# Gate and up products of a SwiGLU by feature instead of by token: activations stream past stationary weights

## The chip, the cores and the metric

The kernel runs on one core of one Trainium2 chip. The metric is the time on the device in microseconds of one execution. Three runs of the kernel before took 2477.77, 2479.46 and 2479.61 us, so the median is 2479.46 us.

## What is computed

A decoder trunk of two layers on 256 tokens of width 2048, all in float32: an RWKV-7 time mixing layer, then an attention layer (here one block of 256 keys), and after each of them a SwiGLU feed-forward part of width 5632 between two layer norms. The change is in the feed-forward part, which runs twice:

```python
def _swiglu(x, w_gate, w_up, w_down):
    return (jax.nn.silu(x @ w_gate) * (x @ w_up)) @ w_down

for layer in range(DEPTH):                      # DEPTH = 2
    mixed = time_mix(h, ...) if layer < 1 else attention(h, ...)
    h = _layernorm(ALPHA * h + mixed, ln1_w[layer], ln1_b[layer])
    h = _layernorm(ALPHA * h + _swiglu(h, ffn_w_gate[layer], ffn_w_up[layer], ffn_w_down[layer]), ln2_w[layer], ln2_b[layer])
```

## The kernel before

**Products in three parts.** The type float32r lets TensorE take a float32 product in one pass, at less than float32's precision. Each operand is therefore split in a high part (a cast to float32r) and a low part (the rest), and a product is three matmuls: high activations by high weights, high by low, low by high. Activations lie in `ahi` and `alo` ([128, 16 k tiles, 256 tokens]), weights come through a ring of four slots, `raw` (from memory), `whi` and `wlo`.

**Jobs and chunks.** A job makes 512 output columns for both tiles of 128 tokens from all k tiles. A chunk is two k tiles of it (256 x 512 weights, 512 KB), so a gate or up job has 8 chunks. For every chunk, SP issues the DMA into `raw` (L343, L344), ACT casts it to `whi` (`split_hi`, L1270), DVE makes `wlo` (`split_lo`, L1713), and TensorE runs `chunk` (L593 to L604): per k tile and token tile three matmuls of 512 columns, L601 to L603, 12 in a chunk and 96 in a job. The stationary operand, which is loaded again for every matmul, is a 128 x 128 tile of activations, and the weights stream past it. ACT may cast chunk c+4 once TensorE is through with chunk c (`chunk_used`); TensorE waits for `split_done`; SP refills a slot of `raw` once its `wlo` is made. Jobs alternate between two sets of accumulators in PSUM (parity 0: banks 0 and 1, parity 1: banks 2 and 3); `bank_free[parity]` hands a set back.

**The feed-forward part** (`ffn`, on TensorE L1118 to L1146, on ACT L1567, on DVE L2135). The width of 5632 is cut in 11 blocks of 512. Each block is a gate job (parity 0), then an up job (parity 1). ACT takes Silu of the gate sums into `gtmp` (L1577, L1588), DVE multiplies it by the up sums in PSUM (`multiply`, L2143). The result has tokens on the partitions, but the product with `w_down` wants features there: `h_transposes` (L1122 to L1128) turns it with 8 transposes of 128 x 128 (L1127) into banks 4 and 5, after the next block's gate job. ACT casts it into `hThi` (`hidden_hi`, L1573) and DVE subtracts for `hTlo` (`hidden_lo`, L2147). The last block's transposes stand inside the first down job. The order on each engine is the order in the code, and blocks 1 to 10 are a hardware loop of 10 rounds.

**The first gate job** (`normed_job`, L1078) starts while the layer norm is still being finished. Its first three chunks (`plain`, L1092 to L1101) are true float32 matmuls from `raw` and `hF`, the normed activations; each shows as two records of TensorE in the trace. `hF` is what ACT writes (L1544) from transposes (L1089), and DVE splits it into `ahi` and `alo` (`split_act`, L2099, L2100). The other five are ordinary chunks. `normed_job` also opens the products for the keys.

Of the kernel before, what the change touches and what calls it, by code (L numbers as in the profile page):

```python
# [23 lines left out]
F32 = mybir.dt.float32  # L24
# [5 lines left out]
P = 128  # L30
# [126 lines left out]
def trunk(nc, x, rows, rwkv_rows, lora, w, consts, ln_rows, y):  # L157
    with ExitStack() as ctx:
# [25 lines left out]
        ahi = sb("ahi", [P, KT, T], F32R)  # L184
        alo = sb("alo", [P, KT, T], F32R)
# [87 lines left out]
        hF = carve(a2t, KT * T, KT, T)  # L273
        gtmp = carve(common, 32 * KB, TT, NB)
# [3 lines left out]
        spare = alo.rearrange("p (s k m) t -> p s k (m t)", s=RING, k=KC)  # L278
# [51 lines left out]
        h_tr, hhi_done, hlo_done = (sem(n) for n in ("h_tr", "hhi_done", "hlo_done"))  # L330
# [259 lines left out]
        def _(pe):  # L590
# [15 lines left out]
            def job(c, u, parity, kt, hi, lo):  # L606

                pe.wait_ge(bank_free[parity], u + 1)
                for ch in range(kt // KC):
                    chunk(c, ch, parity, kt, hi, lo)  # L610

# [466 lines left out]
            def normed_job(n, name):  # L1078
# [13 lines left out]
                def plain(t, ch):  # L1092
# [19 lines left out]
                for ch in range(PLAIN, CJ):  # L1112
                    pe.wait_ge(ln_hi, n * CJ + ch - PLAIN + 1)
                    chunk(c, ch, 0, KT, ahi, alo)
                pe.wait_ge(ln_hi, (n + 1) * CJ)
                job(c + CJ, j // 2, 1, KT, ahi, alo)

            def ffn(layer):  # L1118
# [3 lines left out]
                def h_transposes(i):  # L1122

                    pe.wait_ge(bank_free[1], i + (j0 // 2 + 2 - u0))
                    for f in range(4):
                        for t in range(TT):
                            last = tr(ps[:, 4 + f // 2, (f % 2) * T + t * P:(f % 2) * T + (t + 1) * P], gtmp[:, t, f * P:(f + 1) * P], ident[:])  # L1127
                    last.then_inc(h_tr, 1)  # L1128

                normed_job(2 * layer, f"up{layer}")  # L1130
# [8 lines left out]
                for ch in range(CF):  # L1139
# [3 lines left out]
                    if ch == 1:  # L1143
                        h_transposes(u0 + FB - 1)
# [4 lines left out]
            normed_job(1, "kvq")  # L1149
# [106 lines left out]
        def _(act):  # L1256
            A = nc.scalar.activation

            def split_hi(c, u, n):

                for ch in range(n):
# [305 lines left out]
            def ffn(layer):  # L1567
                c0, _ = PH[f"up{layer}"]
                u0 = layer * FB

                def hidden_hi(i, f0):
                    act.wait_ge(h_tr, i + 1)
                    A(hThi[:, f0, :], ps[:, 4:6, :].rearrange("p a (k t) -> p (a k) t", k=2), ACT.Copy).then_inc(hhi_done, 1)  # L1573
# [3 lines left out]
                A(gtmp, ps[:, 0:2, :], ACT.Silu).then_inc(bank_free[0], 1)  # L1577
# [3 lines left out]
                with act.Fori(0, FB - 1) as i:  # L1581
                    c = i * (2 * CJ) + (c0 + 2 * CJ)
                    u = i * (2 * CJ // RING) + (c0 + 2 * CJ) // RING
                    split_hi(c + RING, u + 1, CJ)

                    act.wait_ge(h_tr, i + (u0 + 1))
                    act.wait_ge(chunk_used, c + CJ)
                    A(gtmp, ps[:, 0:2, :], ACT.Silu).then_inc(bank_free[0], 1)  # L1588
                    hidden_hi(i + u0, bass.ds(i * 4, 4))
                    split_hi(c + (RING + CJ), u + (1 + CJ // RING), CJ)  # L1590
                c = PH[f"down{layer}"][0] + RING
                split_hi(c, c // RING, 1)
                hidden_hi(u0 + FB - 1, slice((FB - 1) * 4, FB * 4))
# [86 lines left out]
        def _(dve):  # L1680
# [26 lines left out]
            def split_lo(c, n, s0=0):  # L1707

                for ch in range(n):
# [425 lines left out]
            def ffn(layer):  # L2135
# [3 lines left out]
                def multiply(c_end, up_seen):  # L2139
# [140 lines left out]
```

## Time and profile before

| | |
|---|---|
| median of three runs | 2479.46 us |
| the profiled execution | 2478.32 us |
| its span, first to last instruction | 2476.4 us |
| TensorE matmul busy | 2444.3 us, 99% of the span, 15550 records |
| TensorE weight load busy | 2002.6 us, 81%, 15550 records |
| VectorE (DVE) busy | 1410.4 us, 57% |
| ScalarE (ACT) busy | 1074.2 us, 43% |
| GpSimd (POOL) busy | 129.9 us, 5% |
| HBM traffic | 440.88 MB, mean 178 GB/s |
| granted TensorE clock | 0.998 of full speed |

The profiled execution took 1.9 us more than its span and 1.1 us less than the median. The recorded duration of a matmul holds its way through the array, and matmuls overlap, so a matmul of 512 columns that is recorded with 389 ns does not cost 389 ns. What it costs is the pitch, the distance from one start to the next. Where a row of the timeline holds several instructions of one line (xN), its length is N-1 pitches and one duration.

### The profile page before, as it was taken

What the parts mean: (1) busy time and instruction counts of PE and PEld (TensorE: products, weight loads), DVE (VectorE), ACT (ScalarE), POOL (GpSimd) and SP (SyncE); (2) the same over time, 40 slices, a digit from 0 to 9 for tenths busy, and PEclk for the clock granted to TensorE, in tenths of its full rate; (3) what the DMA queues carried; (4) which work ended last, traced back from release to release, by engine and by line L of the source; (5) the groups of instructions that cost most, each with busy time, mean ns of one, the idle gap of its engine ahead of it and who ended that gap; (6) DMA issues with size and microseconds to landing.
All of it is one profiled execution on the core that took longest, in us unless ns stands there. A gap on an engine that the chain in (4) does not pass through costs nothing.

```text
span 2476.4 us, 39453 instructions
## 1 busy us (share of the span) xinstructions
PE 2444.3 (99%) x15550; PEld 2002.6 (81%) x15550; DVE 1410.4 (57%) x1743; ACT 1074.2 (43%) x1348; POOL 129.9 (5%) x172
## 2 busy tenths in 40 slices
PE   8999999999999999999999999999999999999997
PEld 6888787877888888888887888888788888888886
DVE  7788566676744444454446644566744444454445
ACT  4454355444444444443334444453544444444332
POOL 2000235420000000000000000000000000000000
PEclk9999999999999999999999999999999999999999
DMA  7556411265666666666665665445566666666654
GB/s 235 188 193 207 126 42 39 70 209 190 192 190 189 188 191 186 189 188 193 194 195 199 204 193 189 140 169 184 178 187 188 193 187 188 186 199 216 192 194 141
DMA packets 225884, 440.88 MB, mean 178 GB/s; under 512 B 13616, under 2 KB 24240, under 8 KB 224672
## 3 DMA queue, kind: packets, MB, share of 16 engines
q1 hardware_dynamic: 221760, 417.38, 54.3%
q0 software_dynamic: 3600, 21.55, 2.6%
q8 instruction: 92, 1.51, 0.3%
q10 hardware_dynamic: 400, 0.18, 0.0%
q14 instruction: 32, 0.26, 0.0%
HBM read 436.96 MB, written 2.10 MB: 177 GB/s over the span
## 4 chain that ended last, share of the span: by engine, by line
PE 95%; DMA 2%; DVE 1%; ACT 1%; issue 1%; POOL 0%; SPq 0%; DVEq 0%; ACTq 0%
PE ps L601 26%; PE ps L603 26%; PE ps L602 26%; PE ps L914 3%; PE ps L1099 1%; PE ps L797 1%; PE ps L807 1%; PE ps L1127 1%; PE ps L629 1%; PE ps L628 1%; PE ps L630 1%; PE ps L904 1%; PE ps L858 1%; PE ps L762 1%; PE ps L941 1%
## 5 line engine op out<-in xcount | busy, mean ns | idle before, releaser
L1270 ACT CAST whi<-raw 128x1024 fp32r<-128x1024 f32 x735 | 772.8, 1052 | 1146.8 <-PE ps L603 1087.9
L1713 DVE TENSOR_TENSOR wlo<-raw,whi 128x1024 fp32r<-128x1024 f32 x549 | 670.3, 1225 | 615.8 <-ACT whi L1270 613.7
L601 PE MATMUL ps<-whi,ahi 128*128 128x512 f32 x2172 | 851.3, 392 | 0.0
L603 PE MATMUL ps<-whi,alo 128*128 128x512 f32 x2172 | 845.6, 389 | 0.0
L602 PE MATMUL ps<-wlo,ahi 128*128 128x512 f32 x2172 | 845.1, 389 | 0.0
L603 PEld LDWEIGHTS ps<-whi,alo 128*128 128x128 f32 x2172 | 407.6, 188 | 85.7
L602 PEld LDWEIGHTS ps<-wlo,ahi 128*128 128x128 f32 x2172 | 407.9, 188 | 84.3 <-issue 1.0
L601 PEld LDWEIGHTS ps<-whi,ahi 128*128 128x128 f32 x2172 | 407.8, 188 | 84.1 <-DVE alo L2100 0.7
L2045 DVE TENSOR_TENSOR wlo<-raw,whi 128x1024 fp32r<-128x1024 f32 x193 | 236.2, 1225 | 249.6 <-ACT whi L1270 247.5
L601 PE MATMUL ps<-whi,hThi 128*128 128x512 f32 x656 | 255.4, 389 | 0.0
L603 PE MATMUL ps<-whi,hTlo 128*128 128x512 f32 x656 | 255.2, 389 | 0.0
L602 PE MATMUL ps<-wlo,hThi 128*128 128x512 f32 x656 | 255.2, 389 | 0.0
L601 PEld LDWEIGHTS ps<-whi,hThi 128*128 128x128 f32 x656 | 123.1, 188 | 25.7
L602 PEld LDWEIGHTS ps<-wlo,hThi 128*128 128x128 f32 x656 | 123.1, 188 | 25.5
L603 PEld LDWEIGHTS ps<-whi,hTlo 128*128 128x128 f32 x656 | 123.1, 188 | 25.4
L914 PE MATMUL ps<-raw,big 128*128 128x256 f32 x256 | 68.0, 398 | 0.6 <-issue 0.5
L577 POOL DMA_DIRECT2D big<-ln_rows x3 | 1.6, 537 | 1113.1 <-PE ps L630 786.9
L914 PEld LDWEIGHTS ps<-raw,big 128*128 128x128 f32 x256 | 44.7, 189 | 8.5 <-issue 1.3
L1544 ACT ACTIVATE a2t<-ps,lnT 128x128 f32<-128x128 f32 x96 | 34.2, 497 | 33.2 <-PE ps L1089 33.2
L1876 DVE TENSOR_TENSOR rec<-ps,big 128x512 f32<-128x512 f32 x40 | 27.6, 689 | 36.4 <-PE ps L797 36.4
L1721 DVE SCALAR_TENSOR_TENSOR big<-big,mixT 128x256 f32<-128x256 f32 x96 | 40.7, 480 | 0.5
L2147 DVE TENSOR_TENSOR hTlo<-ps,hThi 128x1024 f32 (+1 forms) x22 | 26.9, 1225 | 19.5 <-ACT hThi L1573 19.5
(317 smaller groups left out, 1942.3 us busy)
## 6 DMA issues: line engine op xcount, KB each, us to landing
raw<-w_up SPq DMA_DIRECT2D x176, 512.0 KB, 3.6
raw<-w_down SPq DMA_DIRECT2D x176, 512.0 KB, 3.9
raw<-w_gate SPq DMA_DIRECT2D x170, 512.0 KB, 3.6
raw<-w_k SPq DMA_DIRECT2D x32, 512.0 KB, 3.9
raw<-w_r SPq DMA_DIRECT2D x32, 512.0 KB, 4.4
raw<-w_v SPq DMA_DIRECT2D x32, 512.0 KB, 4.1
raw<-w_o SPq DMA_DIRECT2D x32, 512.0 KB, 4.9
raw<-kv_v SPq DMA_DIRECT2D x32, 512.0 KB, 3.7
```

Source lines behind the costliest of these rows:

```text
L601: mm(o, hi[:, k, tok], whi[:, s, k2, :], start=(k == 0), stop=False)
L602: mm(o, hi[:, k, tok], wlo[:, s, k2, :], start=False, stop=False)
L603: last = mm(o, lo[:, k, tok], whi[:, s, k2, :], start=False, stop=(k == kt - 1))
L628: mm(ps[:, 2 + t, :], hi[:, k, tok], wh[:, k2, :], start=False, stop=False)
L914: last = mm(ps[:, 3, t * T:(t + 1) * T], xxT[:, k, t * P:(t + 1) * P], rawf[:, s, k % FK], start=(i == 0), stop=(k == KT - 1), skip_group_ ...
L1270: nc.scalar.copy(whi[:, s], src).then_inc(hi_done, 1)
L1544: ins = A(hF[:, k, t * P:(t + 1) * P], ps[:, 4 + b, k2 * P:(k2 + 1) * P], ACT.Identity, scale=lnT[:, (n * 2) * KT + k:(n * 2) * KT + k + 1 ...
L1713: V.tensor_tensor(wlo[:, s], src, whi[:, s].bitcast(F32), ALU.subtract).then_inc(split_done, 1)
L1721: return V.scalar_tensor_tensor(out=out, in0=xxT[:, k], scalar=mixT[:, m * KT + k:m * KT + k + 1], in1=xT[:, k, 1:T + 1], op0=ALU.mult, op ...
L1876: V.tensor_tensor(Z.rearrange("p l (j c) -> p l j c", c=CHUNK), ps[:, 0:2, 0:4 * CHUNK].rearrange("p l (j c) -> p l j c", c=CHUNK), mask_l ...
L2045: V.tensor_tensor(wl, raw[:, s], wh.bitcast(F32), ALU.subtract).then_inc(split_done, 1)
L2147: V.tensor_tensor(hTlo[:, f0, :], ps[:, 4:6, :].rearrange("p a (k t) -> p (a k) t", k=2), hThi[:, f0, :].bitcast(F32), ALU.subtract).then_ ...
```

## The change

In the gate and up jobs the roles are swapped. The stationary operand becomes a tile of 128 features of the weights, and the activations of all 256 tokens stream past it, so that features come out on the partitions and the transposes go. For this `ahi` and `alo` become two halves of one tensor `ahl` ([128, 16, 2, 256]): for each k tile the high and the low activations lie side by side. Per k tile and each of 4 feature tiles there are two matmuls (`turned_chunk`): `whi` by the run of 512 columns (high and low), and `wlo` by the 256 high columns, added onto the first half of the same bank. High and low sums stand in the two halves of a bank and are added later, so a job now fills four banks (parity 0: 0 to 3, parity 1: 4 to 7). ACT copies the low halves out (`keep_lo`), DVE adds the high halves (`gate_sum`, and the first line of `multiply`), ACT takes Silu in place, DVE multiplies. In the first gate job of each layer four banks are not free yet, so it works with 128 or 256 columns: `narrow_chunk` has three matmuls of 256 columns per feature tile, and `plain` has a float32 matmul of 128 columns per feature tile and token tile. The down, key, value, query, output and RWKV products keep the old form; only their activations lie in `ahl` now.

```diff
-        ahi = sb("ahi", [P, KT, T], F32R)
-        alo = sb("alo", [P, KT, T], F32R)
+        ahl = sb("ahl", [P, KT, 2, T], F32R)
+        ahi, alo = ahl[:, :, 0], ahl[:, :, 1]
...
-        hF = carve(a2t, KT * T, KT, T)
-        gtmp = carve(common, 32 * KB, TT, NB)
+        hF = carve(a2t, 0, KT, 2, T)[:, :, 1]
+        gtmp = carve(common, 32 * KB, FK, T)
+        low_half = carve(big, 80 * KB, FT, T)
...
+            def turned_chunk(c, ch, parity):
+                s = ch % RING
+                pe.wait_ge(split_done, c + (ch + 1))
+                for k2 in range(KC):
+                    k = ch * KC + k2
+                    for f in range(FK):
+                        o, cols = ps[:, 4 * parity + f, :], slice(f * P, (f + 1) * P)
+                        mm(o, whi[:, s, k2, cols], ahl[:, k].rearrange("p n t -> p (n t)"), start=(k == 0), stop=False, skip_group_check=True)
+                        last = mm(o[:, 0:T], wlo[:, s, k2, cols], ahi[:, k, :], start=False, stop=(k == KT - 1), skip_group_check=True)
+                last.then_inc(chunk_used, 1)
...
+            def narrow_chunk(c, ch):
...
+                    for f in range(FK):
+                        o, cols = ps[:, f // 2, (f % 2) * T:(f % 2 + 1) * T], slice(f * P, (f + 1) * P)
+                        mm(o, whi[:, s, k2, cols], ahi[:, k, :], start=False, stop=False, skip_group_check=True)
+                        mm(o, wlo[:, s, k2, cols], ahi[:, k, :], start=False, stop=False, skip_group_check=True)
+                        last = mm(o, whi[:, s, k2, cols], alo[:, k, :], start=False, stop=(k == KT - 1), skip_group_check=True)
...
-                        last = mm(ps[:, t, :], hF[:, k, tok], raw[:, ch, k2, :], start=(k == 0), stop=False)
+                        if by_feature:
+                            for f in range(FK):
+                                last = mm(ps[:, f // 2, (f % 2) * T + t * P:(f % 2) * T + (t + 1) * P], raw[:, ch, k2, f * P:(f + 1) * P], hF[:, k, tok],
+                                          start=(k == 0 and t == 0 and f % 2 == 0), stop=False, skip_group_check=True)
...
                 with pe.Fori(0, FB - 1) as i:
-                    job(i * (2 * CJ) + (c0 + 2 * CJ), i + (j0 // 2 + 1), 0, KT, ahi, alo)
-                    h_transposes(i + u0)
-                    job(i * (2 * CJ) + (c0 + 3 * CJ), i + (j0 // 2 + 1), 1, KT, ahi, alo)
-                    pe.wait_ge(hlo_done, i + (u0 + 1))
+                    turned_job(i * (2 * CJ) + (c0 + 2 * CJ), i + (j0 // 2 + 1), 0)
+                    turned_job(i * (2 * CJ) + (c0 + 3 * CJ), i + (j0 // 2 + 1), 1)
...
-                    if ch == 1:
-                        h_transposes(u0 + FB - 1)
...
+                def keep_lo(c_end, parity, f0, kept):
+                    act.wait_ge(chunk_used, c_end)
+                    nc.scalar.copy(low_half[:, f0, :], ps[:, 4 * parity:4 * parity + FK, T:2 * T]).then_inc(kept, 1)
...
                 with act.Fori(0, FB - 1) as i:
...
-                    split_hi(c + RING, u + 1, CJ)
-                    act.wait_ge(h_tr, i + (u0 + 1))
-                    act.wait_ge(chunk_used, c + CJ)
-                    A(gtmp, ps[:, 0:2, :], ACT.Silu).then_inc(bank_free[0], 1)
-                    hidden_hi(i + u0, bass.ds(i * 4, 4))
-                    split_hi(c + (RING + CJ), u + (1 + CJ // RING), CJ)
+                    keep_lo(c, 1, bass.ds(i * FK, FK), up_lo_kept)
+                    split_hi(c + RING, u + 1, 2)
+                    hidden_hi(i + u0, bass.ds(i * FK, FK))
+                    split_hi(c + RING, u + 1, CJ - 2, 2)
+                    keep_lo(c + CJ, 0, bass.ds(i * FK + FK, FK), gate_lo_kept)
+                    split_hi(c + (RING + CJ), u + (1 + CJ // RING), 2)
+                    act.wait_ge(bank_free[0], i + (j0 // 2 + 3))
+                    A(gtmp, gtmp, ACT.Silu).then_inc(silu_done, 1)
+                    split_hi(c + (RING + CJ), u + (1 + CJ // RING), CJ - 2, 2)
...
-                def multiply(c_end, up_seen):
-                    dve.wait_ge(bank_free[0], up_seen)
-                    dve.wait_ge(chunk_used, c_end)
-                    V.tensor_tensor(gtmp, gtmp, ps[:, 2:4, :], ALU.mult).then_inc(bank_free[1], 1)
+                def multiply(i, f0, ups):
+                    low = low_half[:, f0, :]
+                    dve.wait_ge(up_lo_kept, i + 1)
+                    V.tensor_tensor(low, ps[:, 4:4 + FK, 0:T], low, ALU.add).then_inc(bank_free[1], 1)
+                    dve.wait_ge(bank_free[1], ups)
+                    dve.wait_ge(silu_done, i + 1)
+                    V.tensor_tensor(gtmp, gtmp, low, ALU.mult).then_inc(h_made, 1)
+                def gate_sum(i, f0):
+                    dve.wait_ge(gate_lo_kept, i + (layer * (FB - 1) + 1))
+                    dve.wait_ge(hlo_done, i + (u0 + 1))
+                    V.tensor_tensor(gtmp, ps[:, 0:FK, 0:T], low_half[:, f0, :], ALU.add).then_inc(bank_free[0], 1)
...
                 with dve.Fori(0, FB - 1) as i:
                     c = i * (2 * CJ) + (c0 + 2 * CJ)
-                    multiply(c, i + (j0 // 2 + 2))
-                    split_lo(c + RING, CJ)
-                    hidden_lo(i + u0, bass.ds(i * 4, 4))
+                    multiply(i + u0, bass.ds(i * FK, FK), i + (j0 // 2 + 2))
+                    split_lo(c + RING, 2)
+                    hidden_lo(i + u0, bass.ds(i * FK, FK))
+                    split_lo(c + RING, CJ - 2, 0, 2)
+                    gate_sum(i, bass.ds(i * FK + FK, FK))
                     split_lo(c + (RING + CJ), CJ)
```

`turned_job` waits for `bank_free[parity]` and runs the 8 chunks of a job with `turned_chunk`.

## Rows read from the trace of the kernel before

**Rows 1.** The page, its head and first part: busy time by engine.
```profile
span 2476.4 us, 39453 instructions
PE 2444.3 (99%) x15550; PEld 2002.6 (81%) x15550; DVE 1410.4 (57%) x1743; ACT 1074.2 (43%) x1348; POOL 129.9 (5%) x172
```

**Rows 2.** The page, fourth part: the chain that ended last, by engine.
```profile
PE 95%; DMA 2%; DVE 1%; ACT 1%; issue 1%; POOL 0%; SPq 0%; DVEq 0%; ACTq 0%
```

**Rows 3.** The waits, longest first: engine, line, whom it waited for, us, times, longest.
```profile
ACT whi L1270 <- PE ps L603: 1087.9, 679, 3.1
DVE wlo L1713 <- ACT whi L1270: 614.8, 447, 4.7
```

**Rows 4.** Timeline, TensorE in a steady stretch: start us, length us, engine, line, instruction.
```profile
1000.01 0.39 PE L602 MATMUL ps<-wlo,ahi 128*128 128x512 f32 x1
1000.01 0.19 PEld L603 LDWEIGHTS ps<-whi,alo 128*128 128x128 f32 x1
1000.24 0.39 PE L603 MATMUL ps<-whi,alo 128*128 128x512 f32 x1
...
1007.94 0.39 PE L601 MATMUL ps<-whi,ahi 128*128 128x512 f32 x1
```

**Rows 5.** Timeline, TensorE around the transposes of two blocks that follow each other.
```profile
716.67 1.03 PE L1127 MATMUL ps<-ident,common 128*128 128x128 f32 x8
...
761.09 1.04 PE L1127 MATMUL ps<-ident,common 128*128 128x128 f32 x8
761.88 0.47 PE L601 MATMUL ps<-whi,ahi 128*128 128x512 f32 x1
762.20 0.39 PE L602 MATMUL ps<-wlo,ahi 128*128 128x512 f32 x1
...
764.28 0.39 PE L602 MATMUL ps<-wlo,ahi 128*128 128x512 f32 x1
```

**Rows 6.** One line's instructions, the transposes: count, durations in ns, first and last start.
```profile
L1127 PE MATMUL ps<-ident,common x176: 270/272/275, 672.3 to 2229.4; 128*128 128x128 f32 x176
```

**Rows 7.** Timeline, TensorE, float32 matmuls of 512, 256 and 128 columns.
```profile
251.01 1.02 PE L729 MATMUL ps<-big 128*128 128x512 f32 x2
...
277.63 2.76 PE L914 MATMUL ps<-raw,big 128*128 128x256 f32 x12
...
1546.72 0.38 PE L1172 MATMUL ps<-big 128*128 128x128 f32 x2
1546.94 0.60 PE L1173 MATMUL ps<-big 128*128 128x256 f32 x2
```

**Rows 8.** Groups by line and shape, weight loads: count, busy us, mean ns, idle before.
```profile
L601 PEld LDWEIGHTS ps<-whi,ahi 128*128 128x128 f32 x2172 | 407.8, 188 | 84.1 <-DVE alo L2100 0.7 <-issue 0.2
L1172 PEld LDWEIGHTS ps<-big 128*128 128x128 f32 x32 | 6.0, 189 | 1.0
```

**Rows 9.** Timeline, weight loads ahead of float32 matmuls of 2 columns (L732).
```profile
251.87 0.86 PEld L732 LDWEIGHTS ps<-big 128*128 128x128 f32 x7 [0.24 <-issue]
```

**Rows 10.** Timeline, ACT and DVE at the end of an up job.
```profile
741.75 1.21 DVE L2143 TENSOR_TENSOR common<-common,ps 128x1024 f32<-128x1024 f32 x1
742.24 1.06 ACT L1270 CAST whi<-raw 128x1024 fp32r<-128x1024 f32 x1 [1.67 <-PE ps L603]
743.33 1.23 DVE L1713 TENSOR_TENSOR wlo<-raw,whi 128x1024 fp32r<-128x1024 f32 x1 [0.37 <-ACT whi L1270]
...
744.96 1.05 ACT L1270 CAST whi<-raw 128x1024 fp32r<-128x1024 f32 x1 [1.66 <-PE ps L603]
```

**Rows 11.** The page, sixth part, one row: KB of a DMA and us from issue to landing.
```profile
raw<-w_up SPq DMA_DIRECT2D x176, 512.0 KB, 3.6
```

**Rows 12.** Timeline in the norm before the first gate job: float32 products, first split.
```profile
609.83 5.42 PE L1099 MATMUL ps<-raw,a2t 128*128 128x512 f32 x12 [0.29 <-ACT a2t L1544]
611.21 0.43 DVE L2099 CAST ahi<-a2t 128x512 fp32r<-128x512 f32 x1 [4.78 <-ACT a2t L1544]
611.67 0.69 DVE L2100 TENSOR_TENSOR alo<-a2t,ahi 128x512 fp32r<-128x512 f32 x1
```

More of the change, by code:

```diff
@@ L329, in trunk @@
         xhat_done, ln_tr, ln_aff, ln_hi, h_done = (sem(n) for n in ("xhat_done", "ln_tr", "ln_aff", "ln_hi", "h_done"))
-        h_tr, hhi_done, hlo_done = (sem(n) for n in ("h_tr", "hhi_done", "hlo_done"))
+        gate_lo_kept, up_lo_kept, silu_done, h_made, hhi_done, hlo_done = (
+            sem(n) for n in ("gate_lo_kept", "up_lo_kept", "silu_done", "h_made", "hhi_done", "hlo_done"))
         qk_tr, qkt_set, s_made, nm_set, p_set, p_normed, pt_made, pt_set, o_made, o_kept, ohi_set, olo_set, s_read = (
@@ L610, in job, with turned_job @@
                     chunk(c, ch, parity, kt, hi, lo)
+            def turned_chunk(c, ch, parity):
[8 more added lines that the diff above has]
+                last.then_inc(chunk_used, 1)
+            def turned_job(c, u, parity):
+                pe.wait_ge(bank_free[parity], u + 1)
+                for ch in range(CJ):
+                    turned_chunk(c, ch, parity)
+            def narrow_chunk(c, ch):
+                s = ch % RING
+                pe.wait_ge(split_done, c + (ch + 1))
+                for k2 in range(KC):
+                    k = ch * KC + k2
+                    for f in range(FK):
[3 more added lines that the diff above has]
+                        last = mm(o, whi[:, s, k2, cols], alo[:, k, :], start=False, stop=(k == KT - 1), skip_group_check=True)
+                last.then_inc(chunk_used, 1)
             def last_job(c, u, kt, hi, lo):
@@ L1113, in normed_job @@
                     pe.wait_ge(ln_hi, n * CJ + ch - PLAIN + 1)
-                    chunk(c, ch, 0, KT, ahi, alo)
+                    if by_feature:
+                        narrow_chunk(c, ch)
+                    else:
+                        chunk(c, ch, 0, KT, ahi, alo)
                 pe.wait_ge(ln_hi, (n + 1) * CJ)
-                job(c + CJ, j // 2, 1, KT, ahi, alo)
+                if by_feature:
+                    turned_job(c + CJ, j // 2, 1)
+                else:
+                    job(c + CJ, j // 2, 1, KT, ahi, alo)
             def ffn(layer):
@@ L1120, in ffn @@
                 u0 = layer * FB
[L1122 to L1130, printed above, removed]
+                normed_job(2 * layer, f"up{layer}", True)
                 with pe.Fori(0, FB - 1) as i:
-                    job(i * (2 * CJ) + (c0 + 2 * CJ), i + (j0 // 2 + 1), 0, KT, ahi, alo)
-                    h_transposes(i + u0)
-                    job(i * (2 * CJ) + (c0 + 3 * CJ), i + (j0 // 2 + 1), 1, KT, ahi, alo)
-                    pe.wait_ge(hlo_done, i + (u0 + 1))
+                    turned_job(i * (2 * CJ) + (c0 + 2 * CJ), i + (j0 // 2 + 1), 0)
+                    turned_job(i * (2 * CJ) + (c0 + 3 * CJ), i + (j0 // 2 + 1), 1)
                 c, j = PH[f"down{layer}"]
@@ L1257, in _, with split_hi @@
             A = nc.scalar.activation
-            def split_hi(c, u, n):
-                for ch in range(n):
+            def split_hi(c, u, n, at=0):
+                for ch in range(at, at + n):
                     s = (c + ch if isinstance(c, int) else ch) % RING
@@ L1705, in rsqrt, with split_lo @@
                     newton(dst, src, t)
-            def split_lo(c, n, s0=0):
-                for ch in range(n):
+            def split_lo(c, n, s0=0, at=0):
+                for ch in range(at, at + n):
                     s = (s0 + ch) % RING
```

28 lines of the change are left out of this document (16 added, 12 removed).

## The prediction

> **What bounds the kernel now.** I read the page from its head: TensorE is busy for 99% of the span, DVE for 57%, ACT for 43% [rows 1]. The chain that ended last lies on TensorE for 95% of the span [rows 2], and the longest waits are those of ACT for TensorE to be done with a slot, and of DVE for ACT [rows 3]: the two that prepare the weights are ahead. So the time is a count of TensorE's instructions times their pitch, and the pitch has to be read from starts, since recorded durations overlap.
>
> In a steady stretch 35 pitches lie between the first and the last start of [rows 4]: 7.93 / 35 = 0.2266 us for a float32r matmul of 512 columns. At the granted 2.4 GHz its 512 columns alone are 0.2133 us, so there are **13.3 ns on top**, which I call the overhead. Each such matmul has its own weight load, recorded with 0.19 us, which starts with the matmul before it [rows 4, 8]: the load lies fully beside a stream of 0.213 us. The block period, from one group of transposes to the next, is 761.09 - 716.67 = 44.42 us [rows 5]. Two jobs of 96 matmuls are 192 x 0.22667 = 43.52 us. What is left is 0.90 us; 8 transposes at (1.04 - 0.27) / 7 = 0.110 us are 0.88 of it [rows 5, 6]. Job ends and loop rounds cost TensorE nothing now.
>
> **What goes: the transposes.** All 176 [rows 6], in 22 groups, on the path: 22 x 0.90 = **19.8 us less**. They can't leave a hole that something else fills: what follows each is a matmul whose operands were ready (no idle stands in [rows 5]).
>
> **What is added: more, smaller matmuls.** The columns stay the same. A job before: 96 matmuls of 512, 49152 columns. After: 64 of 512 and 64 of 256, again 49152. But there are 128 matmuls and weight loads for 96, and half of the loads must hide behind a stream of 256 columns, 0.1067 us. 42 of the 44 gate and up jobs change so (all but the first gate job of each layer). No row has a float32r matmul of 256 columns, so its pitch is the unknown of this case, and nearly the whole answer.
>
> *Bounds.* From below: columns at the rate of the 512s, 0.2267 / 2 = 0.1133 us, that is all overhead going with columns. That is also about what a load needs: where matmuls of 2 columns follow each other, 7 loads take 0.86 us, (0.86 - 0.19) / 6 = 0.112 us each [rows 9]. The nearest rows for a load behind a stream of 0.107 us are the float32 matmuls of 128 columns, which stream each column in two cycles: two of them take 1546.94 - 1546.72 = 0.22 us, 0.110 each, with loads recorded as long as those of the float32r ones, 189 against 188 ns [rows 7, 8]. So load and stream still overlap when they are equally long. From above: the overhead is not always 13.3 ns. Behind the transposes, from 762.20 to 764.28, 9 pitches take 2.08 us, 0.2311 each, before they settle at 0.2267 [rows 5]: an overhead of 17.8 ns. If that stayed for every matmul, a 512 would cost 0.2311 and a 256 0.1245 us.
>
> *The value I take.* Float32 matmuls of 256 columns have a pitch of (2.76 - 0.38) / 11 = 0.2164 us for 0.2133 us of stream [rows 7], some 3 ns of overhead, with the same load beside them. So the rest of the 13.3 ns belongs to float32r, which reads a column of four bytes every cycle where float32 has two cycles for it. I read it as a price of each load that runs beside such a stream, since it moves after a change of what is loaded; a price of the load is the same for 256 columns as for 512. Then a 256 costs 0.1067 + 0.0133 = **0.1200 us**. I take the settled 0.2267 for the 512s, because steady stretches hold it over any change of slot and k tile.
>
> A turned job: 64 x (0.2267 + 0.1200) = 22.19 us for 96 x 0.2267 = 21.76, +0.43; 42 x 0.43 = **18.0 us more**. `narrow_chunk`: 24 x 0.1200 = 2.88 us for 12 x 0.2267 = 2.72, and there are 5 in each layer: 10 x 0.16 = **1.6 us more**. `plain`: now each of the two token tiles has 12 records of 512 columns [rows 12], with a pitch of 1.02 - 0.59 = 0.43 us as the two of L729 have it [rows 7] (0.59 is one record's duration), 5.16 us; after, 48 records of 128 columns at 0.110, 5.28. Two token tiles in two layers: **0.5 us more**.
>
> A rule of the Trainium skill (TensorE: Matmul & The Clock Gate, sections "Back-to-back issue gap" and "LDWEIGHTS (loading the stationary operand)") puts a warm matmul at N/2.4 + 2.5 ns and a load of 128 columns at 128/1.2 = 106.7 ns. It speaks softly against the change, as the load becomes as long as the stream of 256. For 512 columns the rule gives 215.8 ns and this trace shows 226.6 [rows 4], so for float32r the row decides. By the rule alone, for old and new matmuls alike, a pair would cost 1.3 ns more than its share of columns does now, 3.4 us in all, and the change would come out about where rival A has it.
>
> **What moves off TensorE.** On ACT a block gets two copies of 1024 elements out of PSUM beside Silu and cast, on DVE two additions. At 1.05 us for each on ACT and 1.23 on DVE, what 1024 elements cost there now, ACT has 20 x 1.05 = 21.0 us and DVE 20 x 1.23 = 24.6 us of work in a block of 44 [rows 10]. The tightest place is the end of an up job, t = 0. ACT casts chunk c+3 (to 1.05), copies the low half (2.1); DVE does `wlo` of c+3 (2.3), then adds (3.5) and, behind its wait for the sum and for Silu, multiplies (4.8). Queued behind these on DVE is `wlo` of chunk c+4, whose cast is ready at 2.72 + 1.05 = 3.8: done at 6.1, and TensorE wants it at 4 x 2.72 = 10.9. SP refills that slot 2.3 us later than now; the DMA lands in 3.6 us [rows 11], at 9.7, and ACT wants it at 13.6. The gate job's end is easier (one copy, one addition). The four new banks of a job are freed by that same addition, a whole job before they are wanted. So I cost all of it at nothing; if the cover were gone, each microsecond late would count at 42 job ends, 42 us. In the norm, `split_act` now writes two runs of 256 in place of one of 512. Its cast has 0.43 us for 512 elements [rows 12], less than the 0.69 of the subtraction; were it as slow as that, 0.26 us per chunk, a chunk would take DVE 0.69 + 0.69 + 1.23 = 2.61 us, still under the 2.72 of TensorE. Nothing.
>
> **Sum.** -19.8 + 18.0 + 1.6 + 0.5 = +0.3 us. The profiled execution would take 2478.3 + 0.3 = 2478.6; the median stands 1.1 above it: **2479.7 us**. One ns on the pitch of the 256s is 42 x 64 + 240 = 2928 matmuls, 2.9 us; the break-even lies at 0.1199.
>
> **Rivals.**
> *A. The overhead goes with the columns.* The 3 ns of float32 are per matmul, the rest is a slower stream: a 256 costs 0.003 + (0.2267 - 0.003) / 2 = 0.1148, a pair 1.5 ns over its share: 2688 x 1.5 = 4.0 us, narrow 0.4, plain 0.5: -14.9, 2464.6 us. With nothing per matmul it is -19.3, 2460.2. For it: 0.112 is all that a load needs. Against it: a slower stream would not explain pitches that differ by 4 ns for equal columns [rows 4, 5]. The Trainium skill's rule above (TensorE: Matmul & The Clock Gate, "Back-to-back issue gap") is this rival's mechanism.
> *B. The overhead stays unsettled (the slower side).* The alternation of 512 and 256 columns never lets the pattern of [rows 4] settle, in the loops of both layers, and every matmul has 17.8 ns: a pair costs 0.2311 + 0.1245 = 0.3556 for 0.3400, 2688 x 0.0156 = 41.9 us, narrow 2.7, plain 0.5: +25.3, 2504.7 us. It is slower by over 0.2% as soon as the mean overhead exceeds some 14.3 ns, one more than now. For it: one break of the pattern in [rows 5] is followed by nine unsettled pitches. Against it: they settle, and on the low side.
> *C. A load isn't hidden behind 256 columns.* Then a 256 costs 0.120 + 0.107: +313 us, 2793 us. Against it: [rows 7].
> *D. A wait at block ends*, 1 us each: about +42 us. Against it: the 4 us of room above.
> That the change doesn't do what it says: ruled out as to the transposes, no line of them is left.
>
> **How the numbers follow.** Forecast 0.38, A 0.31, B 0.26, C 0.02, D 0.03. A measurement of this kernel can tell about 0.2%, 5 us, from no change. The forecast's own spread (an overhead of 12.3 to 15 ns) is 2474 to 2489; of its 0.38, 0.05 is faster, 0.27 within and 0.06 slower. Faster: 0.31 + 0.05 = 0.36. Same: 0.27. Slower: 0.26 + 0.02 + 0.03 + 0.06 = 0.37. The range runs from A's lower end, 2460, to just past B, 2506; C, D, and the outer tails of A and B are left out, under 0.2.
>
> **What would show it.** No line of transposes; groups of float32r matmuls with 512 and with 256 columns, 2688 each in turned jobs. The start-to-start distance of `wlo` matmul and next `whi` matmul is the number that decides: 0.120 for the forecast, 0.113 to 0.115 for A, 0.124 with 0.231 for the 512s for B, 0.227 for C. The block period: 2 x 22.19 = 44.4 us, against 43.7 for A and 45.5 for B. TensorE should sit idle before none of the new matmuls in the loops, and the waits of [rows 3] keep their order, with ACT still waiting for TensorE; if TensorE waits for DVE or ACT, D is right and my margins are wrong.

## The result: 0.8% slower, and the profile after

The changed kernel takes 2498.56 us (median of 4 runs, 2496.84 to 2499.84) where the kernel before takes 2479.5. The ratio is 1.0079, with a 95% interval of 1.0067 to 1.0091, so 19.1 us slower. That lies in the predicted range of 2460 to 2506, in its slower half; the forecast itself was 2479.7, as good as no change.

The page of the changed kernel, its head, busy time by engine, the chain that ended last, and the groups of the new matmuls (count, busy us, mean ns):

```profile
span 2495.7 us, 42513 instructions
PE 2463.2 (99%) x16982; PEld 2070.2 (83%) x16982; DVE 1456.5 (58%) x1785; ACT 1114.7 (45%) x1392; POOL 129.7 (5%) x172
...
PE 94%; DMA 2%; DVE 2%; ACT 1%; issue 1%; POOL 0%; SPq 0%; DVEq 0%; ACTq 0%
...
L622 PE MATMUL ps<-ahl,whi 128*128 128x512 f32 x2688 | 949.9, 399 | 0.0
L623 PE MATMUL ps<-ahl,wlo 128*128 128x256 f32 x2688 | 754.9, 281 | 0.0
```

Against [rows 1, 2] TensorE is as busy as before (99%), holds the chain nearly as before (94%, it was 95%), and has 1432 records more. The two new groups have 2688 matmuls each and no idle before them. ACT and DVE have gained 40 and 46 us of work that shows nowhere in the chain. So the question is again the pitch. TensorE in the middle of the loop of layer 0, starts and lengths in us:

```profile
1000.17 0.40 PE L622 MATMUL ps<-ahl,whi 128*128 128x512 f32 x1
1000.40 0.28 PE L623 MATMUL ps<-ahl,wlo 128*128 128x256 f32 x1
1000.52 0.40 PE L622 MATMUL ps<-ahl,whi 128*128 128x512 f32 x1
1000.76 0.28 PE L623 MATMUL ps<-ahl,wlo 128*128 128x256 f32 x1
...
1001.23 0.40 PE L622 MATMUL ps<-ahl,whi 128*128 128x512 f32 x1
...
1002.29 0.40 PE L622 MATMUL ps<-ahl,whi 128*128 128x512 f32 x1
```

Three pairs take 1001.23 - 1000.17 = 1.06 us, six take 2.12: **353.3 ns a pair**, not the 346.7 of the forecast. In the starts to the nanosecond the six matmuls of three pairs have pitches of 236, 113, 233, 117, 241 and 120 ns, and this round of six repeats, give or take a nanosecond, through all 42 turned jobs. The 320 ns of columns are the same in each, so the overhead is 33.3 ns a pair, 16.7 a matmul, neither the settled 13.3 nor the 17.8 of rival B. Of the first gate job, `narrow_chunk` (L640 to L642) and `plain` (L1134, between the transposes of L1122):

```profile
617.25 0.28 PE L640 MATMUL ps<-ahl,whi 128*128 128x256 f32 x1
617.37 0.28 PE L641 MATMUL ps<-ahl,wlo 128*128 128x256 f32 x1
...
618.93 0.28 PE L642 MATMUL ps<-ahl,whi 128*128 128x256 f32 x1
...
601.56 1.91 PE L1122 MATMUL ps<-ident,common 128*128 128x128 f32 x16
603.80 5.60 PE L1134 MATMUL ps<-a2t,raw 128*128 128x128 f32 x48 [0.34 <-issue]
609.23 1.04 PE L1122 MATMUL ps<-ident,common 128*128 128x128 f32 x8
```

Where all matmuls have 256 columns the pitch is (618.93 - 617.25) / 14 = 0.1200 us, the forecast's number to the digit. The 48 float32 records of a token tile take 609.23 - 603.80 = 5.43 us. The same stretch in the kernel before, with the first transposes of this norm and of the next one:

```profile
600.17 1.91 PE L1089 MATMUL ps<-ident,common 128*128 128x128 f32 x16
602.41 5.39 PE L1099 MATMUL ps<-raw,a2t 128*128 128x512 f32 x12 [0.33 <-issue]
607.63 1.91 PE L1089 MATMUL ps<-ident,common 128*128 128x128 f32 x16
...
1335.05 1.91 PE L1089 MATMUL ps<-ident,common 128*128 128x128 f32 x16
```

It took 607.63 - 602.41 = 5.22 us, so now 0.21 us more, where 0.12 were forecast.

The end of an up job on ACT and on DVE, the place for which the prediction worked out its margins (it answers to [rows 10]; L1606 is `keep_lo`, L2185 the addition, L2188 the multiplication):

```profile
699.33 1.05 ACT L1302 CAST whi<-raw 128x1024 fp32r<-128x1024 f32 x1 [1.78 <-PE ps L623]
700.28 1.01 ACT L1606 COPY big<-ps 128x1024 f32 x1
702.16 1.05 ACT L1302 CAST whi<-raw 128x1024 fp32r<-128x1024 f32 x1 [0.86 <-PE ps L623]
...
700.41 1.23 DVE L1755 TENSOR_TENSOR wlo<-raw,whi 128x1024 fp32r<-128x1024 f32 x1 [1.60 <-ACT whi L1302]
701.55 1.22 DVE L2185 TENSOR_TENSOR big<-ps,big 128x1024 f32 x1
702.81 1.22 DVE L2188 TENSOR_TENSOR common<-common,big 128x1024 f32<-128x1024 f32 x1
703.95 1.22 DVE L1755 TENSOR_TENSOR wlo<-raw,whi 128x1024 fp32r<-128x1024 f32 x1
```

The order is the one worked out. Counted from the cast at 699.33, the `wlo` of chunk c+4 is done after 5.8 us, where 6.1 were forecast. ACT is back waiting for TensorE already before its next cast, and in the turned jobs of both layers (632 to 1106 and 1769 to 2243 us) the trace has no wait of TensorE at all.

**The account.** Turned jobs: 42 x 64 x (0.3533 - 0.3400) = 35.8 us. Narrow chunks: 10 x (24 x 0.1200 - 2.72) = 1.6. Plain: 4 x 0.21 = 0.8. Transposes: -20.0 (read from traces below). Together 18.2 us. The stages of the profile say the same. The norm after the feed-forward part of layer 0 begins here:

```profile
1345.56 1.91 PE L1122 MATMUL ps<-ident,common 128*128 128x128 f32 x16
```

From the first transposes of one norm to those of the next there are 1345.56 - 601.56 = 744.00 us, where the kernel before had 1335.05 - 600.17 = 734.88, so 9.1 us more. In layer 1, from the first transposes to the last matmul, it is 743.77 for 734.64, again 9.1. That is nearly all of the 19.3 us between the two profiled spans. Another 1.4 us lie ahead of the change: the norm before layer 0's first gate job begins at 601.56 us instead of 600.17. And the attention layer between is 0.3 us shorter. Over the other profiles of this study that norm begins anywhere from 599.58 to 605.09, so the 1.4 us are scatter of the part before.

### The profile page after: what moved, and what is told of

It reads as the page before. It is cut to its first block, busy times and chain, and to the rows that moved or that the text cites. A ratio compares the mean times of both kernels' runs of the same rounds, so it can differ in the third digit from the quotient of the medians.

```text
span 2495.7 us, 42513 instructions
## 1 busy us (share of the span) xinstructions
PE 2463.2 (99%) x16982; PEld 2070.2 (83%) x16982; DVE 1456.5 (58%) x1785; ACT 1114.7 (45%) x1392; POOL 129.7 (5%) x172
## 4 chain that ended last, share of the span: by engine, by line
PE 94%; DMA 2%; DVE 2%; ACT 1%; issue 1%; POOL 0%; SPq 0%; DVEq 0%; ACTq 0%
PE ps L622 25%; PE ps L604 13%; PE ps L603 13%; PE ps L605 13%; PE ps L623 13%; PE ps L947 3%; PE ps L830 1%; PE ps L1134 1%; PE ps L840 1%; PE ps L663 1%; PE ps L662 1%; PE ps L661 1%; PE ps L937 1%; PE ps L891 1%; PE ps L795 1%; DMA raw<-w_o 1%
## 5 line engine op out<-in xcount | busy, mean ns | idle before, releaser
L622 PE MATMUL ps<-ahl,whi 128*128 128x512 f32 x2688 | 949.9, 399 | 0.0
L623 PE MATMUL ps<-ahl,wlo 128*128 128x256 f32 x2688 | 754.9, 281 | 0.0
L622 PEld LDWEIGHTS ps<-ahl,whi 128*128 128x128 f32 x2688 | 505.1, 188 | 126.0
L623 PEld LDWEIGHTS ps<-ahl,wlo 128*128 128x128 f32 x2688 | 507.8, 189 | 0.0
L603 PE MATMUL ps<-whi,ahl 128*128 128x512 f32 x788 | 310.2, 394 | 0.0
L605 PE MATMUL ps<-whi,ahl 128*128 128x512 f32 x788 | 306.9, 389 | 0.0
L604 PE MATMUL ps<-wlo,ahl 128*128 128x512 f32 x788 | 306.6, 389 | 0.0
L605 PEld LDWEIGHTS ps<-whi,ahl 128*128 128x128 f32 x788 | 147.9, 188 | 31.2
L603 PEld LDWEIGHTS ps<-whi,ahl 128*128 128x128 f32 x788 | 148.0, 188 | 30.8 <-issue 0.2
L604 PEld LDWEIGHTS ps<-wlo,ahl 128*128 128x128 f32 x788 | 148.0, 188 | 30.5 <-issue 0.5
```

Source lines behind the costliest of these rows:

```text
L603: mm(o, hi[:, k, tok], whi[:, s, k2, :], start=(k == 0), stop=False)
L604: mm(o, hi[:, k, tok], wlo[:, s, k2, :], start=False, stop=False)
L605: last = mm(o, lo[:, k, tok], whi[:, s, k2, :], start=False, stop=(k == kt - 1))
L622: mm(o, whi[:, s, k2, cols], ahl[:, k].rearrange("p n t -> p (n t)"), start=(k == 0), stop=False, skip_group_check=True)
L623: last = mm(o[:, 0:T], wlo[:, s, k2, cols], ahi[:, k, :], start=False, stop=(k == KT - 1), skip_group_check=True)
```

## The experiments

Theory 1: an overhead of 13.3 ns for each float32r matmul, settled where lengths are equal, unsettled where they alternate. Rivals: it comes from what is read (weights as the stationary operand, high and low side by side), from two matmuls in a row that accumulate in one bank with different extents, or, later, from the length of the load. The kernel before took 2479.17 us beside the first four kernels, 2478.37 beside the next four, 2479.47 and 2478.64 beside the last ones. "A pair" is the work of one `whi` by 512 and one `wlo` by 256, as the mean over the turned jobs from the starts. The diffs of this section are shortened; words such as "512 columns" stand for operands.

### Runs of eight, and of four

```diff
                 for k2 in range(KC):
                     k = ch * KC + k2
                     for f in range(FK):
-                        mm(o, whi[...], ahl[:, k] as 512 columns, ...)
-                        last = mm(o[:, 0:T], wlo[...], ahi[:, k, :], ...)
+                        mm(o, whi[...], ahl[:, k] as 512 columns, ...)
+                for k2 in range(KC):
+                    k = ch * KC + k2
+                    for f in range(FK):
+                        last = mm(o[:, 0:T], wlo[...], ahi[:, k, :], ...)
```

> The changed kernel with one edit: in each chunk of a turned job the eight matmuls of 512 columns come first, then the eight of 256, so that lengths change twice in a chunk and not 16 times. Theory 1, the overhead unsettles because lengths alternate: in the changed kernel a pair costs 353.3 ns (233 to 241 and 113 to 120), uniform ones 226.7 and 120.0; with runs of eight most of the 6.7 ns a pair should come back, at most 2688 x 6.7 = 18 us, so 2481 to 2490 us. Theory 2, the overhead comes from what is read (the weights as the stationary operand, high and low activations side by side): the order changes nothing, 2498 us. Theory 3, it comes from two matmuls in a row that accumulate in the same bank with different extents: all of it comes back, 2481 us.

> As the run of eight, but in runs of four: per k tile four matmuls of 512 columns, then four of 256. Theory 1 (each change of length costs something until it settles): between the changed kernel and the run of eight, 2485 to 2495 us. Theory 2: 2498 us. Theory 3 (same bank with different extents): the same time as the run of eight, about 2481 us.

Runs of eight: 2485.76 us, 1.0027 of before (1.0016 to 1.0038), 349.2 ns a pair. Runs of four: 2490.45 us, 1.0046 (1.0029 to 1.0062), 350.8 ns a pair. The rows of the timeline for runs of eight (x8 is seven pitches and a duration):

```profile
999.64 1.77 PE L621 MATMUL ps<-ahl,whi 128*128 128x512 f32 x7
1001.25 1.11 PE L625 MATMUL ps<-ahl,wlo 128*128 128x256 f32 x8
```

The eight of 256 have (1.11 - 0.28) / 7 = 0.119 us, nearly all of them 0.120. The first of 512 after them have 233, 236, 229, 232 and 231 ns, then 227, and the last unsettled pitches after the transposes at 761.09 [rows 5] are the same within a nanosecond (233, 236, 228, 233, 231, 226). The same instructions with the same operands in another order are 13 us faster: theory 2 falls. Eight and four differ: theory 3 falls. Both times lie in the range that theory 1 gave.

### Alternating lengths, but another bank

```diff
-                    for f in range(FK):
+                    for n in range(FK):
+                        f = n
                         mm(512 columns into bank f)
+                        f = (n - 1) % FK
                         last = mm(256 columns into bank f)
```

> The changed kernel, lengths still alternate, but each 256 goes to the bank of another feature tile than the 512 before it (512 of tile f, 256 of tile f-1). Theory 1 and theory 2: pairs stay at 353.3 ns, 2498 us. Theory 3 (same bank): pairs fall to 346.7 ns, 2481 us.

2495.57 us in one run, and 353.3 ns a pair, with the same round of six (236, 114, 232, 118, 240, 120). The bank has nothing to do with it. The profiled execution of the changed kernel took 2497.52 us, 1.95 more, and all of that lies ahead of the first norm (it begins at 599.58 us here, at 601.56 there).

### The kernel before without transposes

```diff
                     job(..., 0, KT, ahi, alo)
-                    h_transposes(i + u0)
                     job(..., 1, KT, ahi, alo)
...
-                    A(hThi[:, f0, :], ps[:, 4:6, :]..., ACT.Copy).then_inc(hhi_done, 1)
+                    A(hThi[:, f0, :], gtmp..., ACT.Copy).then_inc(hhi_done, 1)
```

> The kernel before without its 176 transposes and nothing in their place: ACT casts and DVE splits the product as it stands, tokens on the partitions, so the down products get operands in the wrong order. The prediction's first term says 22 x 0.90 = 19.8 us less than before: 2459.7 us. If something else were waiting behind the transposes, less would be gained, 2465 us or more.

ACT's cast and DVE's subtraction also stand at another place in their order, behind the first two chunks. 2458.58 us, 20.6 us less than before, ratio 0.9918 (0.9901 to 0.9934); 19.8 us were predicted. In the traces each of the two feed-forward parts is 10.0 us shorter (from 601.16 to 1326.06 us, 724.90, where the kernel before has 734.88), **20.0 us** in all. Nothing moved into their place.

### All lengths 256

```diff
-                        mm(o, whi[...], ahl[:, k] as 512 columns, ...)
+                        mm(o[:, 0:T], whi[...], ahi[:, k, :], ...)
+                        mm(o[:, T:2 * T], whi[...], alo[:, k, :], ...)
                         last = mm(o[:, 0:T], wlo[...], ahi[:, k, :], ...)
```

> The changed kernel with its run of 512 columns cut in two: whi by the 256 high columns, whi by the 256 low ones, wlo by the 256 high ones, so all turned matmuls have 256 columns and each its own weight load. Theory 1 (13.3 ns for every float32r matmul with its load, settled where lengths are equal): 3 x 120.0 = 360 ns for a pair's work, 6.7 more than 353.3, so 2498.6 + 2688 x 0.0067 = 2516 us. Theory 2 (the overhead goes with columns or with what is read): less than 353 ns, 2498 us or below.

2518.8 us in one run (2516 were expected; its first norm begins 3.5 us late), and 360.0 ns for the three, 120.0 each. That is theory 1's number. So one matmul of 512 columns is better than two of 256: the third load and matmul costs 6.7 ns a pair more than even the dear alternation.

### High and low activations apart

```diff
-        ahl = sb("ahl", [P, KT, 2, T], F32R)
-        ahi, alo = ahl[:, :, 0], ahl[:, :, 1]
+        ahl = sb("ahl", [P, 2, KT, T], F32R)
+        ahi, alo = ahl[:, 0], ahl[:, 1]
...
-  ahl[:, k] as one run of 512 columns
+  ahl[:, :, k], two runs of 256
```

> The changed kernel with the high and low activations in two separate regions again, so that the matmul of 512 columns reads two runs of 256 which lie 16 KB apart. Theory 1 (only lengths and their order count): 353.3 ns a pair, 2498 us. Theory 2 (one contiguous run of 512 matters): above 353.3 ns; each ns more is 2.7 us.

2498.5 us in one run, 353.3 ns a pair, the same round of six. That the two lie side by side in memory makes no difference here.

### Mirrored, and runs of sixteen

```diff
                     for f in range(FK):
-                        512 columns of f, then 256 columns of f
+                        f even: 512 columns, then 256; f odd: 256 columns, then 512
```

> The changed kernel with every second feature tile in the other order: 512, 256, 256, 512, so that lengths change half as often, in runs of two. Theory 1: between the changed kernel (353.3 ns a pair) and the runs of four, 2490 to 2498 us. Theory 2: 353.3 ns, 2498 us.

> The mirrored order again (512, 256, 256, 512), timed in rounds: one look gave 2486.8 us and 348.3 ns a pair. From the pitches 2498.6 - 2688 x 0.0050 = 2485 us, so still slower than before by 0.2 to 0.3%. If order were a matter of chance in that look, it comes back at 2498 us.

> The changed kernel with eight of 512 then eight of 256 in even chunks and the reverse in odd ones, so runs of sixteen. If a change of length costs something until the overhead settles (349.2 ns a pair in runs of eight, 346.7 settled), half as many changes give 347.9 ns a pair: 2485.8 - 2688 x 0.00125 = 2482.4 us. If runs of eight have some other floor, 2485.8 us. In neither case is it below the 2479 of before: 346.7 ns for every pair would give 2480 us.

The mirrored order took 2486.81 us in a single run, and 2483.92 as the median of 10, 1.0015 of before (1.0006 to 1.0025), with 348.3 ns a pair both times (the single run began its first norm 3.0 us later): less than runs of four or of eight, where 2490 to 2498 us had been expected at first. So the number of changes of length does not settle it alone. Runs of sixteen took 2482.21 us, 1.0008 (0.9998 to 1.0017), 347.9 ns a pair, as the expectation had worked out: no difference from before can be told.

### Other sizes

The middle k tiles of the down products in the kernel before, most of their sums left out:

```diff
-                        o, tok = ps[:, 2 * parity + t, :], slice(t * P, (t + 1) * P)
-                        mm(o, hi[:, k, tok], whi[:, s, k2, :], ...)
+                        m, n = (64, 512), (32, 512) in layer 0, (128, 384), (128, 128) in layer 1
+                        o, tok = ps[0:m, 2 * parity + t, 0:n], slice(t * P, t * P + m)
+                        mm(o, hi[:, k, tok], whi[:, s, k2, 0:n], ...)
```

> The kernel before, with smaller matmuls in the middle k tiles of the down products (the first and the last k tile stay whole, most of the sums are left out): in layer 0 stationary tiles of 64 token columns in the first job and 32 in the second, 512 columns streaming; in layer 1 whole stationary tiles with 384 streaming columns in the first job and 128 in the second. If the 13.3 ns on top of a stream is the weight load's hold on it (it grows with the length of the load): 226.7 falls to about 220 with 64 and 217 with 32. If it is a fixed price of a float32r matmul: 226.7 stays, whatever the stationary size. In both, 384 columns give 160 + 13.3 = 173.3 ns; for 128 columns the load binds, about 112 to 120 ns, where the stream alone would be 53 + 13 = 67.

The timeline of each of the four kinds, first and last row of a stretch (10, 10, 7 and 10 rows with those left out), and last a stretch of the whole matmuls that were kept (7 rows):

```profile
1104.75 0.39 PE L608 MATMUL ps<-whi,hTlo 128*64 128x512 f32 x1
...
1106.83 0.39 PE L608 MATMUL ps<-whi,hTlo 128*64 128x512 f32 x1
...
1160.84 0.40 PE L606 MATMUL ps<-whi,hThi 128*32 128x512 f32 x1
...
1162.92 0.39 PE L606 MATMUL ps<-whi,hThi 128*32 128x512 f32 x1
...
2235.95 0.33 PE L608 MATMUL ps<-whi,hTlo 128*128 128x384 f32 x1
...
2236.99 0.33 PE L608 MATMUL ps<-whi,hTlo 128*128 128x384 f32 x1
...
2278.91 0.28 PE L608 MATMUL ps<-whi,hTlo 128*128 128x128 f32 x1
...
2279.92 0.27 PE L608 MATMUL ps<-whi,hTlo 128*128 128x128 f32 x1
...
2324.24 0.63 PE L607 MATMUL ps<-wlo,hThi 128*128 128x512 f32 x1
...
2326.80 0.63 PE L607 MATMUL ps<-wlo,hThi 128*128 128x512 f32 x1
```

384 columns: 1.04 / 6 = 0.1733 us, 160.0 and 13.3. 128 columns: 1.01 / 9 = 0.112 us, the price of a load in [rows 9]. But 64 stationary columns give 2.08 / 9 = 0.231 us over this stretch (230.0 ns over the job), 32 give 2.08 / 9 = 0.231 (231.7 over the job): **more** than the 226.7 with all 128, in every job that has them, and never settling at 226.7. Neither reading of the expectation had that. The loads of 64 and 32 columns are recorded with 134 and 109 ns, whole ones with 188. So a shorter load doesn't shorten the overhead.

In this run the granted clock fell from 2.4 to 1.2 GHz at 2290 us, after 11.7 us of matmuls with 128 columns in which TensorE waited once, 0.6 us for DVE. The first eight rows above lie before the fall. The last two lie behind it: at 1.2 GHz a whole matmul of 512 columns takes (2326.80 - 2324.24) / 6 = 0.4267 us, which is its 512 columns and nothing on top. So the 13.3 ns stand beside a matmul at the full clock and not in this stretch at half of it.

### Other kinds

The same place again, now into banks that nobody reads, lengths in turn by position:

```diff
+                        short, narrow = ((512, bfloat16), (256, bfloat16)) in layer 0, ((256, float32r), (384, float32r)) in layer 1
+                        for e in range(3 * TT):
+                            n = (512, short)[e % 2]
+                            mm(ps[:, 6 + e // 3, 0:n], a, b[:, 0:n], start=True, stop=True)
```

> The kernel before with the middle k tiles of its down products replaced by matmuls into unused banks, so that the sums miss them: in layer 0 both operands read as bfloat16, in the first job all of 512 streaming columns, in the second 512 and 256 in turn; in layer 1 float32r as before, with activations as the stationary operand as before the change, in the first job 512 and 256 in turn, in the second 512 and 384 in turn. Theory 1 (the overhead belongs to float32r's stream of four bytes a column, and unsettles where lengths alternate, whichever operand stands still): bfloat16 gives 213.3 plus about 3 ns for 512, the same for 256, steady when they alternate; float32r gives 353.3 ns for a pair of 512 and 256 as in the changed kernel, and more than 400 ns (320 + 53.3 + 2 x 13.3) for 512 and 384. Theory 2 (the swap of roles matters): 346.7 ns for the pair of 512 and 256. If the overhead is the same for bfloat16, it is not a price of float32r.

```profile
1125.13 0.10 PEld L607 LDWEIGHTS ps<-wlo,hThi 128*128 128x128 bf16 x1
1125.13 0.38 PE L607 MATMUL ps<-whi,hThi 128*128 128x512 bf16 x1
...
1126.21 0.38 PE L607 MATMUL ps<-whi,hTlo 128*128 128x512 bf16 x1
...
1185.01 0.38 PE L607 MATMUL ps<-whi,hThi 128*128 128x512 bf16 x1
1185.22 0.27 PE L607 MATMUL ps<-wlo,hThi 128*128 128x256 bf16 x1
...
1186.31 0.38 PE L607 MATMUL ps<-whi,hTlo 128*128 128x512 bf16 x1
...
2212.26 0.40 PE L607 MATMUL ps<-whi,hTlo 128*128 128x512 f32 x1
...
2213.65 0.40 PE L607 MATMUL ps<-wlo,hThi 128*128 128x512 f32 x1
...
2309.83 0.40 PE L607 MATMUL ps<-whi,hTlo 128*128 128x512 f32 x1
...
2311.95 0.40 PE L607 MATMUL ps<-whi,hTlo 128*128 128x512 f32 x1
```

bfloat16: 1.08 / 5 = 0.216 us for 512 columns, and a pair of 512 and 256 takes 1.30 / 4 = 0.325 us, 216 and 109 ns in turn without exception: some 2.5 ns each on top of the columns, and alternating costs nothing. The overhead of 13.3 ns and its restlessness are float32r's. A bfloat16 load is recorded with 0.10 us for 0.19, but the float32r load of 32 columns is nearly as short and has the overhead all the same. Whether it belongs to float32r's stream or to having such a load at all no run can tell.

The Trainium skill (TensorE: Matmul & The Clock Gate, section "Back-to-back issue gap") gives the gap of warm matmuls taken by themselves, without a budget for their loads, as N/2.4 + 2.5 ns. The bfloat16 rows, each with a load of its own, agree within 0.2 ns (215.8 and 109.0), the float32r rows are 10.8 ns above it where lengths are equal.

float32r with the old roles: 353.3 ns a pair in the third job (2309.83 to 2311.95, six pairs in 2.12), as with the new roles. But in the first job, 2212.26 to 2213.65, four pairs take 1.39 us, **346.7 to 347 ns**: pitches of 231, 112, 233, 117, 231, 113, 232 and 118 ns, and again through the job. The same instructions have two steady patterns. What differed between the two jobs is the group of 8 transposes in the first, after its second chunk: ahead of it, even that job ran the dear pattern (113, 233, 117, 241, 120, 236). For 512 and 384 in turn it was 203.3 ns a matmul in both jobs, 406.7 a pair, again 16.7 ns a matmul on top of the columns.

### One break

`turns` is 8 in the first turned job of layer 0, 7 in that of layer 1, and 0 in all others.

```diff
                 for ch in range(CJ):
                     turned_chunk(c, ch, parity)
+                    if ch == 1:
+                        for n in range(turns):
+                            tr(ps[:, 3, n % 4 * P:(n % 4 + 1) * P], ident[:], ident[:])
```

> The changed kernel with one break of the pattern per layer and nothing else: after the second chunk of the first turned job, 8 transposes of the identity into an idle bank in layer 0, 7 in layer 1 (their result is never read). In the run with the mixed kinds, 512 and 256 in turn took 346.7 ns a pair after a group of 8 transposes and 353.3 ns elsewhere, each kept up to the end of its job. Theory 4, there are two steady patterns for the same matmuls and only the phase at the start chooses: a layer whose break hits the cheap one keeps it through its 21 turned jobs and gains 1344 x 6.7 = 8.9 us, so 2480.6 + 1.6 us for the breaks if both do, about 2490 if one does. If the cheap pattern was due to the swapped roles or the down products' surroundings and not to the phase: 353.3 ns everywhere, 2500 us.

2481.21 us (10 runs, 2479.64 to 2483.02), 1.0010 of before (1.0000 to 1.0020): 17.4 us less than the changed kernel (16.5 when each is set against the kernel before that ran beside it), for 15 transposes more. Around the break of layer 0, and 360 us later:

```profile
636.90 0.40 PE L622 MATMUL ps<-ahl,whi 128*128 128x512 f32 x1
637.14 0.28 PE L623 MATMUL ps<-ahl,wlo 128*128 128x256 f32 x1
637.25 0.40 PE L622 MATMUL ps<-ahl,whi 128*128 128x512 f32 x1
637.49 0.28 PE L623 MATMUL ps<-ahl,wlo 128*128 128x256 f32 x1
637.61 1.03 PE L633 MATMUL ps<-ident 128*128 128x128 f32 x8
...
1000.06 0.39 PE L622 MATMUL ps<-ahl,whi 128*128 128x512 f32 x1
1000.29 0.28 PE L623 MATMUL ps<-ahl,wlo 128*128 128x256 f32 x1
...
1002.14 0.39 PE L622 MATMUL ps<-ahl,whi 128*128 128x512 f32 x1
```

Up to the break the job runs the dear round (233, 118, 241, 120, 236, 113), behind it the cheap one. Six pairs take 1002.14 - 1000.06 = 2.08 us, 346.7 ns each, in pitches of 230, 116, 230 and 117 ns in layer 0 (and in another round of the same price, 231, 112, 233, 117, in layer 1). Each of the 42 jobs but the two with the break takes 22.19 us, where all took 22.61. The cheap pattern survives job ends, loop rounds and a change of every address, and the dear one does so too. Theory 4 holds in this: the same matmuls keep one of two prices, and what ran once before them decides which. The expectation had 2482.2 us for a cheap pattern in both layers.

## Why the prediction held, and where it was off

**The number.** That the measured time lies in the range says little: the range was wide enough to take in rivals A and B, and the forecast of +0.3 us missed 19 us.

**What bounds it: right.** TensorE without idle time in the loops, before and after, and everything was decided by pitches.

**The transposes: right.** 19.8 us predicted; with them gone and nothing in their place the medians differ by 20.6 and the traces by 20.0.

**The moved work at nothing: right.** The rows of ACT and DVE show the order worked out, and TensorE waits for neither in the loops. Rival D is out, and so is C: a load of 112 ns hides behind 107 ns of stream and 13 of overhead.

**The pitch of 256 columns: right, 0.1200 us**, in `narrow_chunk` and with all lengths at 256. Rival A, overhead that goes with the columns, is out: 512, 384 and 256 columns all have 13.3 ns on top. The reason I gave is shown in part. The overhead is float32r's and goes by matmul: bfloat16 has 2.5 ns, and float32 some 3 ns with loads as long as float32r's [rows 7, 8]. That it is a price of the load is not shown, since every float32r matmul in every run has a load of its own, and it does not grow with the load's length: 64 and 32 stationary columns have more of it. The rule N/2.4 + 2.5 ns, which the prediction called rival A's mechanism, shares with A the small price per matmul, not the slower stream; bfloat16 follows it here and float32r does not.

**The settled 512s: the step that failed.** The prediction says "I take the settled 0.2267 for the 512s, because steady stretches hold it over any change of slot and k tile". That is true of uniform stretches and was carried to alternating ones. The term was +18.0 us and measured +35.8: 353.3 ns a pair for 346.7. Rival B named the mechanism, alternating lengths keep the overhead from settling, and had the direction right; it mis-sized it, with 17.8 ns a matmul for the measured 16.7, and the reason was too simple. Alternating lengths do settle, at one of two prices, and the changed kernel happens to enter the dear one in both layers. Nor is the row that B rested on the rule: the nine unsettled pitches stand behind the transposes at 761.09, while behind those at 716.67 there are only 233 and 230 ns before 227. The forecast's 346.7 is what the same kernel has at the cheap price: with one break it takes 2481.2 us, 1.6 of them for the two breaks, where 2479.7 were forecast. That the forecast comes true there is in part luck, since nothing in it foresaw two prices.

**Plain: mis-sized.** 0.8 us for 0.5, as the 48 records of 128 columns follow each other at (5.60 - 0.27) / 47 = 0.113 us and not at 0.110.

What stays open is why. No run shows what in the chip sets the 13.3 ns (only that they were absent in the stretch at 1.2 GHz), what the patterns are locked to, or how to tell ahead which one a program enters. That 8 and 7 transposes both led to a cheap pattern may be luck; nothing else was tried. No run tried a break in the kernel before; its uniform matmuls already have the settled 13.3 ns.

No variant beats the kernel before. At 346.7 ns a pair a turned job takes 22.19 us. The old one takes 21.76 and half of 0.90 for its transposes, 22.21. The 32 more instructions in a job cost 32 x 13.3 = 427 ns, and its four transposes of 109 ns gave 436.

## What to carry to other kernels

Count instructions, not columns, when tiles are cut anew: here every float32r matmul costs at least 13.3 ns on top of its columns at the full clock, while its load is hidden, so 32 more matmuls in a job weigh as much as four transposes of 128 x 128. Where a loop mixes lengths in float32r, look at the starts over some dozen matmuls rather than at one row, and try another order or one break before the loop: the same work differed by some 16 us here, in one kernel. For a change that trades like for like, price the remainder before writing it; the best variant of this one was a draw.

## What the runs showed that I had not expected

- Float32r with 512 and 256 columns in turn settles at one of two prices, 353.3 or 346.7 ns a pair, and keeps the one it enters for over 460 us.
- Mirrored (512, 256, 256, 512) it takes 348.3 ns a pair, less than in runs of eight (349.2) or of four (350.8).
- Stationary tiles of 64 and 32 columns have longer pitches (230.0 and 231.7 ns for 512 streaming columns) than whole ones (226.7).
- A bfloat16 matmul of 512 columns takes 215.8 ns here, and alternating with 256 does not disturb it.
- At a granted clock of 1.2 GHz a float32r matmul of 512 columns took 426.7 ns, its columns alone.
